# The second mixer's attention scores: one fp32 product against two fp32r products on high and low parts

## The reference

```
q  = rms_norm(q, q_norm_g)                    # 8 heads of 64; 2 key/value heads
kc = rms_norm(compress(k_cmp), k_norm_g[0])   # 8 compressed keys (blocks of 32 tokens)
s      = einsum(q, kc) * 64**-0.5             # compressed scores, softmax over 8 keys
s_sel  = einsum(q, rms_norm(k_sel, k_norm_g[1])) * 64**-0.5    # all 4 blocks are selected: 256 keys
s_win  = einsum(q, rms_norm(k_win, k_norm_g[2])) * 64**-0.5    # a window of 512 holds all 256 keys
o = g0 * softmax(s) @ vc + g1 * softmax(mask(s_sel)) @ v_sel + g2 * softmax(mask(s_win)) @ v_win
```

## Time and profile before

| | us |
|---|---|
| median of 3 runs | 1504.49 (1504.27 to 1506.66) |
| the profiled execution's own time | 1502.06 |
| its span, first to last instruction | 1500.0 |
| PE busy | 1464.5 (98% of the span) |
| DVE busy | 1143.5 (76%) |
| ACT busy | 771.0 (51%) |
| POOL busy | 142.2 (9%) |
| mean granted TensorE clock | 0.992 of 2.4 GHz |

### The profile page before, as it was taken

How to read it: one execution, slowest core, us unless ns; L and a number is a source line. 1 busy time by engine, 2 the same in 40 slices (tenths; PEclk the granted TensorE clock), 3 DMA queues, 4 the chain that set the end, 5 groups by cost and what they waited for, 6 DMA issues and landing times.

```text
span 1500.0 us, 24413 instructions
## 1 busy us (share of the span) xinstructions
PE 1464.5 (98%) x8543; PEld 1271.6 (85%) x8543; DVE 1143.5 (76%) x1830; ACT 771.0 (51%) x1257; POOL 142.2 (9%) x140
## 2 busy tenths in 40 slices
PE   6999999999999999999999999999999999999998
PEld 5888889888888888889988888898877789888887
DVE  4777777878778777787787777868699877567776
ACT  5443465663434634347655434467578665453432
POOL 0000015100000000003220000011333210000000
PEclk9999999999999999999999999999999999999999
DMA  7666655546565666665455655556322256546662
GB/s 290 204 196 186 192 165 173 154 154 192 199 187 189 218 196 197 194 186 168 141 169 188 199 187 190 169 183 228 108 72 85 73 158 187 187 155 197 195 189 78
DMA packets 71072, 261.74 MB, mean 174 GB/s; under 512 B 8016, under 2 KB 8016, under 8 KB 70736
## 3 DMA queue, kind: packets, MB, share of 16 engines
q1 hardware_dynamic: 69696, 253.79, 52.6%
q10 hardware_dynamic: 1296, 6.85, 1.3%
HBM read 259.56 MB, written 1.05 MB: 174 GB/s over the span
## 4 chain that ended last, share of the span: by engine, by line
PE 89%; DVE 4%; ACT 3%; issue 2%; POOL 1%; DMA 0%; ACTq 0%; DVEq 0%
PE work L732 25%; PE work L733 12%; PE acc L470 8%; PE acc L472 8%; PE acc L471 8%; PE work L470 8%; PE work L472 7%; PE work L471 7%; DVE wlo L456 1%; PE work L1459 1%; ACT whi L449 1%; PE acc L1488 0%; PE work L660 0%; DVE frac L1869 0%; PE acc L660 0%
## 5 line engine op out<-in xcount | busy, mean ns | idle before, releaser
L456 DVE TENSOR_TENSOR wlo<-raw,whi 128x1024 fp32r<-128x1024 f32 x460 | 550.3, 1223 | 189.3 <-ACT whi L449 187.7
L732 PE MATMUL work<-xboth,whi 128*128 128x512 f32 x1600 | 560.7, 393 | 0.0
L449 ACT ACTIVATE whi<-raw 128x1024 fp32r<-128x1024 f32 x480 | 475.8, 1040 | 53.1 <-PE work L472 35.8
L733 PE MATMUL work<-xboth,wlo 128*128 128x256 f32 x1600 | 445.3, 278 | 0.0
L732 PEld LDWEIGHTS work<-xboth,whi 128*128 128x128 f32 x1600 | 299.7, 187 | 68.5
L733 PEld LDWEIGHTS work<-xboth,wlo 128*128 128x128 f32 x1600 | 301.2, 188 | 4.3
L812 ACT ACTIVATE sg<-sg 128x256 f32<-128x256 f32 x100 | 41.8, 418 | 476.1 <-DVE sg L853 476.1
L472 PE MATMUL acc<-whi,hlo 128*128 128x512 f32 x440 | 173.8, 395 | 0.0
L471 PE MATMUL acc<-wlo,hhi 128*128 128x512 f32 x440 | 173.6, 395 | 0.0
L470 PE MATMUL acc<-whi,hhi 128*128 128x512 f32 x440 | 173.5, 394 | 0.0
L470 PE MATMUL work<-xboth,whi 128*128 128x256 f32 x488 | 143.2, 293 | 0.0
(11 more groups left out here) (433 smaller groups left out, 2069.6 us busy)
## 6 DMA issues: line engine op xcount, KB each, us to landing
raw<-stream SPq DMA_DIRECT2D x480, 512.0 KB, 3.7
par<-pm ACTq DMA_DIRECT2D x2, 1644.5 KB, 7.1
pfa<-pf_a ACTq DMA_DIRECT2D x3, 516.0 KB, 3.6
pfb<-pf_b ACTq DMA_DIRECT2D x2, 516.0 KB, 7.9
x<-x_in SPq DMA_DIRECT2D x2, 512.0 KB, 5.8
out<-x SPq DMA_DIRECT2D x2, 512.0 KB, 2.6
par<-pm ACTq DMA_DIRECT2D x1, 820.0 KB, 4.2
pre<-pf_a ACTq DMA_DIRECT2D x1, 4.0 KB, 4.0
```

What stands on the lines that cost most here:

```text
L449: nc.scalar.activation(chunk(whi, place, c)[:, cols], chunk(raw, place, c)[:, cols], ACT.Copy).then_inc(hi_ready, 1)
L456: nc.vector.tensor_tensor(chunk(wlo, place, c)[:, cols], chunk(raw, place, c)[:, cols], chunk(whi, place, c)[:, cols].bitcast(F32), ALU.su ...
L732: nc.tensor.matmul(o[:, :], hi[:, k * P:(k + 1) * P], xboth[:, k, :], start=k == 0, stop=False)
L733: m = nc.tensor.matmul(o[:, 0:S], lo[:, k * P:(k + 1) * P], xhi[:, k, :], start=False, stop=k == KD - 1)
```

## The change

The query is written twice side by side (`qd`, 128 tokens x 8 heads x 2 x 64), so that one transpose gives it in rows 0 to 63 and again in rows 64 to 127 of a bank. ACT copies all 128 rows to `qT` with the type fp32r (the high part), and DVE overwrites rows 64 to 127 with bank minus high part, the low part. The keys are doubled in the same way, but ACT's copy of the high part stays in both halves of `kT`, and DVE writes the low part to `klo`, 64 rows. A score is then `qT` (high over low, 128 rows) times `kT` (high twice) plus the upper half of `qT` (high) times `klo`: high*high + low*high + high*low, in two fp32r products. The compressed key gets the same (`kcT`, `kclo`).

With it: the query's root is multiplied in the second of its two steps, which writes the doubled form; `kcn` is written twice; DVE, not ACT, empties the banks of qt, kt and kct, after ACT's copy (`qk_hi`); `e6` stands before `kct` on PE and ACT, so that these two exchange banks; `split_lo` of the two chunks stands ahead of the qt subtractions and of the kct subtraction on DVE. `qd` lies in the s5 buffer `rotated`, `cc` and `cvt` lie in `maskadd` and `upper`.

```diff
--- before.py
+++ after.py
@@ -161,9 +161,9 @@
 
 ROUNDS = 16
 BANKED2 = (["q0", "q1"] + [f"kvc{i}" for i in range(4)] + ["ng", "u0", "u1", "u2", "kv0", "kv1", "u3", "hid0", "e0", "e1", "hid1", "e2",
-           "e3", "hidt0", "hidt1", "e4", "cmp0", "cmp1", "e5", "qt00", "qt01", "qt10", "qt11", "kt0", "kt1", "kct", "e6", "cs0", "cs1", "e7"])
+           "e3", "hidt0", "hidt1", "e4", "cmp0", "cmp1", "e5", "qt00", "qt01", "qt10", "qt11", "kt0", "kt1", "e6", "kct", "cs0", "cs1", "e7"])
 BANK2 = {name: k % 4 for k, name in enumerate(BANKED2)}
-BY_DVE2 = ["cmp1", "cs0", "cs1", "bu0"]
+BY_DVE2 = ["cmp1", "qt00", "qt01", "qt10", "qt11", "kt0", "kt1", "kct", "cs0", "cs1", "bu0"]
 BY_ACT2 = BANKED2[:BANKED2.index("hid0")] + ["e0", "hid0", "e1", "e2", "hid1"]
 BY_ACT2 += [name for name in BANKED2[BANKED2.index("e3"):] if name not in BY_DVE2]
 JOBS2 = ["q0", "kv0"] + [name for name in BANKED2[BANKED2.index("hidt0"):] if name[0] != "e"]
...
+        klo = m1("klo", [HD, 4, S], F32R)
+        qd = rotated[:, :, :, :, :].rearrange("p t a b n -> p t (a b n)")
...
@@ -1427,24 +1429,26 @@
                     begin2(pe, name)
                     for a in range(4):
                         h = 4 * b + a
-                        m = nc.tensor.transpose(bank2(name, slice(a * P, (a + 1) * P))[0:HD], xn[:, t, h * HD:(h + 1) * HD], ident[:, :])
+                        m = nc.tensor.transpose(bank2(name, slice(a * P, (a + 1) * P)), qd[:, t, h * P:(h + 1) * P], ident[:, :])
                     done(name, m)
             qn_ready.wait(pe, 2 * T)
             for t in range(T):
                 name = f"kt{t}"
                 begin2(pe, name)
                 for a in range(4):
-                    m = nc.tensor.transpose(bank2(name, slice(a * P, (a + 1) * P))[0:HD], xn[:, t, 512 + a * HD:512 + (a + 1) * HD], ident[:, :])
+                    m = nc.tensor.transpose(bank2(name, slice(a * P, (a + 1) * P)), xn[:, t, a * P:(a + 1) * P], ident[:, :])
                 done(name, m)
+            early(6)
             begin2(pe, "kct")
             kcn_ready.wait(pe, 1)
-            done("kct", nc.tensor.transpose(bank2("kct", slice(0, 16))[0:HD], kcn[0:16, :], ident[0:16, 0:16]))
-            early(6)
-            evac2.wait(pe, BY_ACT2.index("kct") + 1)
+            done("kct", nc.tensor.transpose(bank2("kct", slice(0, 16)), kcn[0:16, :, :].rearrange("p i n -> p (i n)"), ident[0:16, 0:16]))
+            vec2.wait(pe, BY_DVE2.index("kct") + 1)
             for t in range(T):
                 begin2(pe, f"cs{t}")
                 for h in range(8):
-                    m = nc.tensor.matmul(bank2(f"cs{t}", slice(h * 8, h * 8 + 8)), qT[:, h, t * P:(t + 1) * P], kcT[:, (h // 4) * 8:(h // 4) * 8 + 8], start=True, stop=True)
+                    cols = slice((h // 4) * 8, (h // 4) * 8 + 8)
+                    nc.tensor.matmul(bank2(f"cs{t}", slice(h * 8, h * 8 + 8)), qT[:, h, t * P:(t + 1) * P], kcT[:, cols], start=True, stop=False)
+                    m = nc.tensor.matmul(bank2(f"cs{t}", slice(h * 8, h * 8 + 8)), qT[0:HD, h, t * P:(t + 1) * P], kclo[:, cols], start=False, stop=True)
                 done(f"cs{t}", m)
             early(7)
             uhl_ready.wait(pe, 4)
@@ -1456,7 +1460,9 @@
                 if r == 0:
                     masks.wait(pe, 2)
                 for b in range(2):
-                    nc.tensor.matmul(bank2(f"sc{r}", slice(b * S, b * S + nkeys(t))), qT[:, h, t * P:(t + 1) * P], kT[:, 2 * b + h // 4, 0:nkeys(t)], start=True, stop=False)
+                    o = bank2(f"sc{r}", slice(b * S, b * S + nkeys(t)))
+                    nc.tensor.matmul(o, qT[:, h, t * P:(t + 1) * P], kT[:, 2 * b + h // 4, 0:nkeys(t)], start=True, stop=False)
+                    nc.tensor.matmul(o, qT[0:HD, h, t * P:(t + 1) * P], klo[:, 2 * b + h // 4, 0:nkeys(t)], start=False, stop=False)
                     m = nc.tensor.matmul(bank2(f"sc{r}", slice(b * S + t * P, b * S + (t + 1) * P)), identr[:, :], maskr[:, :], start=False, stop=True)
                 done(f"sc{r}", m)
 
@@ -1709,18 +1715,18 @@
                     copy("hidt1", pcT[:, :, :].rearrange("p b (h n) -> p b h n", h=8), src.unsqueeze(2).broadcast_to([P, 2, 8, 16]))
             early(4)
             job2.wait(act, JOB2["cmp0"])
-            copy("cmp0", kcn[0:16, :], bank2("cmp0", slice(0, HD))[0:16])
+            copy("cmp0", kcn[0:16, 0, :], bank2("cmp0", slice(0, HD))[0:16])
             early(5)
             for t in range(T):
                 for b in range(2):
                     job2.wait(act, JOB2[f"qt{t}{b}"])
-                    copy(f"qt{t}{b}", qT[:, 4 * b:4 * b + 4, t * P:(t + 1) * P], bank2(f"qt{t}{b}")[0:HD].rearrange("p (a n) -> p a n", a=4))
+                    qk_hi.inc(nc.scalar.activation(qT[:, 4 * b:4 * b + 4, t * P:(t + 1) * P], bank2(f"qt{t}{b}").rearrange("p (a n) -> p a n", a=4), ACT.Copy))
             for t in range(T):
                 job2.wait(act, JOB2[f"kt{t}"])
-                copy(f"kt{t}", kT[:, :, t * P:(t + 1) * P], bank2(f"kt{t}")[0:HD].rearrange("p (a n) -> p a n", a=4))
+                qk_hi.inc(nc.scalar.activation(kT[:, :, t * P:(t + 1) * P], bank2(f"kt{t}").rearrange("p (a n) -> p a n", a=4), ACT.Copy))
+            early(6)
             job2.wait(act, JOB2["kct"])
-            copy("kct", kcT[:, :], bank2("kct", slice(0, 16))[0:HD])
-            early(6)
+            qk_hi.inc(nc.scalar.activation(kcT[:, :], bank2("kct", slice(0, 16)), ACT.Copy))
             for t in range(T):
                 csm.wait(act, t + 1)
                 cexp.inc(nc.scalar.activation(ce[:, t], ce[:, t], ACT.Exp))
@@ -1902,8 +1908,8 @@
             nrm.wait(dve, 1)
             for t in range(T):
                 q3 = xn[:, t, 0:512].rearrange("p (h n) -> p h n", h=8)
-                step(tt(q3, q3, bc(qk_rstd[:, t * 12:t * 12 + 8], HD), ALU.mult))
-                qn_ready.inc(stt(out=q3, in0=q3, scalar=HD ** -0.5, in1=par[:, PN["q_g"]].unsqueeze(1).broadcast_to([P, 8, HD]), op0=ALU.mult, op1=ALU.mult))
+                step(stt(out=q3, in0=q3, scalar=HD ** -0.5, in1=par[:, PN["q_g"]].unsqueeze(1).broadcast_to([P, 8, HD]), op0=ALU.mult, op1=ALU.mult))
+                qn_ready.inc(tt(qd[:, t, :].rearrange("p (h i n) -> p h i n", h=8, i=2), q3.unsqueeze(2).broadcast_to([P, 8, 2, HD]), bc(qk_rstd[:, t * 12:t * 12 + 8], P).rearrange("p h (i n) -> p h i n", i=2), ALU.mult))
             split_lo(dve, place, [16])
 
             for w in range(2):
@@ -1933,7 +1939,8 @@
                 step(tt(k3, k3, bc(qk_rstd[:, t * 12 + 8:t * 12 + 12], HD), ALU.mult))
                 for b in range(2):
                     kb = k3[:, 2 * b:2 * b + 2, :]
-                    ins = tt(kb, kb, par[:, PN["k_g"]][:, (b + 1) * HD:(b + 2) * HD].unsqueeze(1).broadcast_to([P, 2, HD]), ALU.mult)
+                    ins = tt(xn[:, t, b * S:(b + 1) * S].rearrange("p (h i n) -> p h i n", h=2, i=2), kb.unsqueeze(2).broadcast_to([P, 2, 2, HD]),
+                             par[:, PN["k_g"]][:, (b + 1) * HD:(b + 2) * HD].unsqueeze(1).unsqueeze(1).broadcast_to([P, 2, 2, HD]), ALU.mult)
                     if b == 0:
                         step(ins)
                     else:
@@ -1964,14 +1971,30 @@
             split_lo(dve, place, range(32, E_CHUNK[4] + 7))
 
             evac2.wait(dve, BY_ACT2.index("cmp0") + 1)
-            step(tt(sq[0:16, 0, 0:HD], kcn[0:16, :], kcn[0:16, :], ALU.mult))
+            step(tt(sq[0:16, 0, 0:HD], kcn[0:16, 0, :], kcn[0:16, 0, :], ALU.mult))
             step(nc.vector.tensor_reduce(kc_st[0:16, 0:1], sq[0:16, 0, 0:HD], AX.X, ALU.add))
             s5m.inc(ts(kc_st[0:16, 0:1], kc_st[0:16, 0:1], 1.0 / HD, EPS, ALU.mult, ALU.add))
             nrm.wait(dve, 3)
             job2.wait(dve, JOB2["cmp1"])
             emptied("cmp1", tt(vcs, bank2("cmp1", slice(0, HD)).unsqueeze(1).broadcast_to([P, 8, HD]), bc(mask8[:, :], HD), ALU.mult))
-            kcn_ready.inc(stt(out=kcn[0:16, :], in0=kcn[0:16, :], scalar=kc_st[0:16, 1:2], in1=par[0:16, PN["k_g"]][:, 0:HD], op0=ALU.mult, op1=ALU.mult))
-            split_lo(dve, place, range(E_CHUNK[5] + 6, E_CHUNK[6] + 7))
+            for i in (1, 0):
+                ins = stt(out=kcn[0:16, i, :], in0=kcn[0:16, 0, :], scalar=kc_st[0:16, 1:2], in1=par[0:16, PN["k_g"]][:, 0:HD], op0=ALU.mult, op1=ALU.mult)
+                if i:
+                    step(ins)
+                else:
+                    kcn_ready.inc(ins)
+            split_lo(dve, place, [E_CHUNK[5] + 6])
+            for i, (t, b) in enumerate((t, b) for t in range(T) for b in range(2)):
+                qk_hi.wait(dve, i + 1)
+                o = qT[HD:P, 4 * b:4 * b + 4, t * P:(t + 1) * P]
+                emptied(f"qt{t}{b}", tt(o, bank2(f"qt{t}{b}")[HD:P].rearrange("p (a n) -> p a n", a=4), o.bitcast(F32), ALU.subtract))
+            for t in range(T):
+                qk_hi.wait(dve, 2 * T + t + 1)
+                cols = slice(t * P, (t + 1) * P)
```

(4 more changed lines are left out.)

14 lines of the change are left out of this document (7 added, 7 removed).

## The result

The changed kernel takes 1519.75 us (median of 4 runs, 1515.51 to 1522.37), the kernel before, on the same chip, 1505.41 (4 runs, 1504.27 to 1506.66): ratio 1.0096, 95% interval 1.008 to 1.0111. It is slower, and the forecast of 1507.0 with its range to 1512 was too low. The profiled execution is the one of 1515.51; its span is 1513.6, against 1500.0 before.

What follows compares the result with a forecast made beforehand. TensorE was taken to bound the kernel overall (PE 98% busy), but DVE rounds 4 to 13. Terms 5.8 - 0.3 - 1.8 - 1.7 + 0.5 = +2.5 us on 1502.06, plus 2.4 to the median, gave 1507.0, range 1501.5 to 1512.

Steps and rivals of the forecast that it cites:

- Step 1: Ahead of the stage: longer query and key normalisations on DVE delay POOL's chain and what follows, +0.6 us.
- Step 2: Before kt0: banks freed by DVE instead of ScalarE, so e6 starts 2.9 us later, the first 0.6 included.
- Step 3: Behind e6: the compressed key's high and low parts wait in queues, so compressed scores start another 2.9 us later.
- Step 4: Compressed scores: 32 fp32r products replace 16 fp32 ones of 32 records, -0.3 us.
- Step 5: Rounds' score products: 10.4 us less TensorE work, 3.5 counting: -1.8 in rounds 0 to 3, -1.7 in 14 and 15.
- Step 6: Granted clock in the stage: a fifth of the cost of e6 running at 1.2 GHz, +0.5 us, the unsure term.
- the lower clock spreads over the stage: Rival, between query transposes and round 0: idling brings 1.2 GHz before e6, price 2.3 to 4.8 us, say 1510; chance 0.30.
- TensorE counts in every round: Rival, in the rounds: the whole 10.4 us TensorE saving counts, sum -4.9, 1499.6 us; chance 0.14 with cheaper second and third terms.
- an fp32 product holds less to save: Rival, in the score products: weight loading stays, so rounds save 1.3 and 0.9, sum +3.8, 1508.3 us; chance 0.11.

Runs made afterwards that it cites:

- Number 8: Kernel before, with four 128x512 maxima on DVE ahead of the second evacuation of the compressed branch; TensorE idles 5.7 us longer, round 0's scores come 6.3 later.
- Numbers 6: Changed kernel with low parts in 128 rows, query, key and compressed-key subtractions ahead of weight splits, kct's copy earlier on ScalarE; ten runs 1503.5 to 1508.4 us.
- number 7: Changed kernel with low parts in 128 rows, e6 in a free bank behind the queries, kct before the keys, weight splits behind all subtractions; ratio 0.9975 to before.
- number 1: Changed kernel with klo and kclo in 128 rows, lower half zero, so every score product reads all of qT; 1511.98 us.
- numbers 3: Changed kernel with all compressed products over 64 rows, low query times high compressed key left out; products 0.11 us apart, total time not in the text.
- 4: Changed kernel with score products reordered, every other pair 64-row first, so changes between 128 and 64 rows are halved; 1515.67 us.
- number 2: Changed kernel with only kclo in 128 rows, klo left as it was; by the ratios 0.24% or 3.6 us gained, compressed scores 6.9 us.
- 11: Kernel before, scores left in fp32, with e6 moved between the queries' first and second chunk into its own bank; 1505.84 us, ratio 1.0000.
- 15: Kernel before, unedited, traced once more; the traced run took 1506.14 us.
- number 13: Changed kernel, unedited, traced once more; the traced run took 1514.81 us.
- number 9: Changed kernel with low parts in 128 rows, plus 20 unread products ahead of the keys and 20 ahead of the compressed scores; median 1508.47 us.
- number 5: Kernel before with queries, keys and compressed key typed fp32r, all low parts left out; rounds 1.6 us shorter than before's first trace, total time not in the text.

## Why the prediction was wrong

**Step 1 (+0.6)**: POOL's chain starts 0.2 later. Small, right side.

**Step 2 (e6 +2.9)**: the wait was 2.57 us (2 forecast), kt0 came at 1061.61 (1061.45 forecast), e6 3.5 later. The two multiplies of the compressed key took 1.79 us where 1.34 stood in the sum; the second ended at 1059.6 with POOL's operation (1058.48 + 1.04). So the exclusive lock of the Trainium skill ("SBUF — State Buffer", "SBUF: two separate sides"), which the prediction priced at 0.6 and left out, should have been in the sum. Number 8 shows it four times in a row. From kt0 to e6 it took 1.59 us, not 1.20, since the eight key transposes stand 0.21 apart at 1.2 GHz.

**Step 3 (+2.9)**: 2.59 of idling, 2.8 from e6's end. Right. Numbers 6 and 7 show that both waits can be removed by order and banks, with the arithmetic as it is.

**Step 4 (-0.3) failed, and is the largest miss: +5.6.** It said "now 32 fp32r ones of the same count" and "Bounds -0.6 and +1.0". The products took 9.7 us. Two things were in none of the bounds: the turn between 128 and 64 rows (0.30 against 0.21 apart at 1.2 GHz; numbers 1, 3 and 4 show it by three different edits), and that all of them would run at the lower level. The turn is what a spacing taken from products of one kind can't show; by 0.21 they would be 6.9 us, as in number 2, and at 2.4 GHz 3.6, as in number 7. The 4.1 before, too, had its last 0.8 us at the lower level (from 1066.0); wholly at 2.4 GHz the fp32 products take 3.7 (numbers 8, 11 and 15). So of the 5.6 us above before, 2.8 is the turns and 3.3 the clock, less the 0.4 that the clock cost before; the arithmetic saves 0.1, not 0.3. In the changed kernel's second trace (number 13) the clock's part is 1.2 smaller.

**Step 5 (-3.5) failed too: it had the mechanism right and the size of its products wrong.** TensorE was to be busy 10.4 us less in the rounds. From round 0's maximum to round 15's it was busy 113.0 us, against 112.1 and, in the second trace, 114.8 before. A branch of an even round, and the start of its second:

```profile
1111.18 0.30 PE L1464 MATMUL work<-kT,qT 128*128 128x128 f32 x1
1111.42 0.32 PE L1465 MATMUL work<-klo,qT 64*128 64x128 f32 x1
1111.67 0.33 PE L1466 MATMUL work<-maskr,identr 128*128 128x128 f32 x1
1111.84 0.28 PE L1464 MATMUL work<-kT,qT 128*128 128x128 f32 x1
```

It takes 0.66 where 0.48 was forecast and 0.68 stood before; those of the odd rounds took 0.73 to 0.80 instead of 0.42. The bound of 0.26 for a 64-row product, taken from the place where an fp32 one followed the mask, was the nearer one: both its sides are turns. With the turns gone (number 1) TensorE is busy 101.4, an odd round's branches take 0.40 and 0.35, and the rounds gain 4.3 us, against 3.5 forecast. With the turns they are 1.3 longer than in before's first trace, with two of the stretches at 1.2 GHz in the rounds twice as long (1127.6 to 1134.4 and 1161.7 to 1168.5, against 3.4 us each). In before's own second trace these stretches are as long, and its rounds are 2.2 longer than in its first. Against that trace the changed rounds are 0.9 shorter. So the turns took most of the gain, and not more; the rest is the clock's.

**Step 6 (+0.5) was too low.** The level fell ahead of e6 (1059.3 to 1066.1, +1.3 on e6) and for the whole of the compressed scores (1069.6 to 1083.2, +3.3, of which before had 0.4), and e7 got 1.1 back: 3.1 in all. This is the rival "the lower clock spreads over the stage", given 0.30. Its reason, the two idle stretches, is not shown: number 9 fills them and loses the first fall, but numbers 3, 6 and 7 have that fall before the wait for the keys or without it. That rival alone, at 1510, is still too low: it and the turns together make the result. The rival "TensorE counts in every round" falls with number 1: with 10.7 us of TensorE work less in the rounds they shrink by 4.3. The rival "an fp32 product holds less to save" falls with number 5: a 256-column product takes 0.31 where the fp32 one took 0.62, and that beside a turn.

In sum, of the 13.6 us: e6 starts 3.5 later (steps 1 and 2) and takes 1.3 more (clock), the wait behind it 2.8 (step 3), the compressed scores 5.6 (turns 2.8, clock 2.9, saved 0.1), e7 -1.1, to round 0's scores 12.1; the rounds 1.3, more by the clock and less by the arithmetic, and 0.2 about them. This is the account of one trace of each kernel, the changed one's from its fastest run. Open is what brings the level down ahead of e6, what decides, from one run to the next, how long a stretch at the lower level is, and what the changed kernel's runs above 1519 hold.

## What to carry to other kernels

When a product is split in parts, give the parts the same rows, with zeros if need be, or order them so that like stands by like: a product of more rows cost nothing here, a turn 0.05 to 0.15 us more than products of one kind. When an operand needs one more operation on a second engine, that operation goes ahead of everything in the queue that nobody waits for, and the bank it holds is then not one that TensorE needs next. A price for a new form of instruction taken from rows of one form only can be too low; count also how it stands beside its neighbours. Trace the unchanged kernel more than once before a difference of 1 or 2 us is laid to the change: here its own rounds differed by 2.2.
